# Dense tiles of a hybrid decoder step: the three products as the outermost loop

## What is computed

```python
for layer in range(DEPTH):
    h = rmsnorm(x, norm_mix[layer])
    mix = even_mixer(h, ...) if layer % 2 == 0 else odd_mixer(h, ...)   # each: h @ w_in, mixing, @ w_out
    x = x + mix
    h = rmsnorm(x, norm_mlp[layer])
    x = x + jnp.square(jax.nn.relu(h @ mlp_w_up[layer])) @ mlp_w_down[layer]
y = rmsnorm(x, norm_final)
```

## Time and profile before

| | us |
|---|---|
| median of 3 runs | 3569.35 |
| lowest and highest | 3564.08, 3569.45 |
| the profiled execution | 3563.22 |
| its span, first to last instruction | 3561.4 |
| TensorE busy | 3150.5 (88%) |
| DVE busy | 1233.3 (35%) |
| ACT busy | 742.8 (21%) |
| GpSimd busy | 248.5 (7%) |

### The profile page before, as it was taken

One profiled execution on the slowest core, in us unless ns is written; L12 is line 12 of the kernel. 1 busy time (PEld: TensorE's weight loads), 2 busy tenths in 40 slices (PEclk: granted clock), 3 DMA queues, 4 the chain that ended last, 5 costly groups with the idle time before them and its releaser, 6 DMA issues. The chain is left out here.

```text
span 3561.4 us, 45192 instructions
## 1 busy us (share of the span) xinstructions
PE 3150.5 (88%) x18272; PEld 2946.8 (83%) x18272; DVE 1233.3 (35%) x1537; ACT 742.8 (21%) x1029; POOL 248.5 (7%) x303
## 2 busy tenths in 40 slices
PE   7997788987428899999998999699869899999997
PEld 6996667765318899999998999577649899999996
DVE  5633444325322422222224221644261422222223
ACT  3212211104221311112122000321140311111112
POOL 1001211101000100000001000323000100000000
PEclk9998777767659999999999999666569999999998
DMA  4110000010002111111112111000112111111111
GB/s 133 41 53 12 1 1 0 0 29 24 10 15 92 33 49 46 47 47 47 42 48 82 47 47 36 1 1 0 36 65 95 42 47 42 47 47 47 46 48 48
DMA packets 222442, 141.92 MB, mean 40 GB/s; under 512 B 6419, under 2 KB 218722, under 8 KB 221861
## 3 DMA queue, kind: packets, MB, share of 16 engines
q1 hardware_dynamic: 222380, 141.08, 13.1%
HBM read 120.06 MB, written 21.10 MB: 40 GB/s over the span
## 5 line engine op out<-in xcount | busy, mean ns | idle before, releaser
L161 PE MATMUL ps<-act_hi,w_hi 128*128 128x344 f32 x3072 | 662.0, 324 | 89.9 <-DVE act_lo L382 33.5
L161 PE MATMUL ps<-act_lo,w_hi 128*128 128x344 f32 x3072 | 656.5, 322 | 0.0
L161 PE MATMUL ps<-act_hi,w_lo 128*128 128x344 f32 x3072 | 653.1, 321 | 0.0
L161 PEld LDWEIGHTS ps<-act_hi,w_hi 128*128 128x128 f32 x3072 | 520.7, 189 | 99.4 <-issue 83.5
L161 PEld LDWEIGHTS ps<-act_lo,w_hi 128*128 128x128 f32 x3072 | 524.3, 190 | 0.0
L161 PEld LDWEIGHTS ps<-act_hi,w_lo 128*128 128x128 f32 x3072 | 516.3, 189 | 0.0
L143 ACT ACTIVATE w_hi<-w_raw 128x1024 fp32r<-128x1024 f32 x192 | 202.6, 1055 | 1163.1 <-PE ps L161 1096.5
L567 DVE TENSOR_TENSOR proj<-proj,ps 128x1032 f32 (+1 forms) x80 | 98.4, 1230 | 704.6 <-PE ps L161 704.6
L161 PE MATMUL ps<-hidden_lo,w_hi 128*128 128x344 f32 x1536 | 325.9, 320 | 0.0
L161 PE MATMUL ps<-hidden_hi,w_hi 128*128 128x344 f32 x1536 | 325.8, 320 | 0.0
L161 PE MATMUL ps<-hidden_hi,w_lo 128*128 128x344 f32 x1536 | 324.3, 319 | 0.0
(11 more groups left out here) (322 smaller groups left out, 3156.8 us busy)
## 6 DMA issues: line engine op xcount, KB each, us to landing
w_raw<-mlp_w_up SPq DMA_DIRECT2D x64, 512.0 KB, 4.0
w_raw<-mlp_w_down SPq DMA_DIRECT2D x64, 512.0 KB, 3.6
w_raw<-gla_w_in SPq DMA_DIRECT2D x24, 512.0 KB, 3.8
w_raw<-even_w_in SPq DMA_DIRECT2D x22, 512.0 KB, 3.8
x_save<-proj SPq DMA_DIRECT2D x2, 4128.0 KB, 12.2
proj<-x_save SPq DMA_DIRECT2D x2, 4128.0 KB, 12.8
x_rows<-x_prompt SPq DMA_DIRECT2D x8, 512.0 KB, 3.5
w_raw<-even_w_out SPq DMA_DIRECT2D x8, 512.0 KB, 3.7
```

Source lines behind the costliest of these rows:

```text
L161: last = c.nc.tensor.matmul(c.ps[:, 3 * slot + ch, 0:CW], w[:, slot, k, :], x[:, k, ch * CW:(ch + 1) * CW], start=(k == 0 and n == 0), sto ...
```

## The change

In `multiply_tile` the product becomes the outermost loop, then `k`, then the column chunk. The order of the products becomes high by high, low weights by high activations, high weights by low activations. `ready` is given the pass `n` along with `k`, and its last call is `ready(2, KT)`.

In the norm, `ready` waits in the first pass for `act_hi[k]` (`norm_upper`), does nothing in the second, and in the third issues the sums of squares and waits for `act_lo[k]`, as it did before in the only pass.

In a down tile, `ready` waits in the first pass for seven `hid_hi` at k = 0 and for the eighth at k = 7, and at the start of the third pass for all eight `hid_lo`.

```diff
@@ multiply_tile
-    for k in range(KT):
-        if ready:
-            ready(k)
-        for n, (w, x) in enumerate(((c.w_hi, hi), (c.w_hi, lo), (c.w_lo, hi))):
+    for n, (w, x) in enumerate(((c.w_hi, hi), (c.w_lo, hi), (c.w_hi, lo))):
+        for k in range(KT):
+            if ready:
+                ready(n, k)
             for ch in range(NCH):
                 last = c.nc.tensor.matmul(c.ps[:, 3 * slot + ch, 0:CW], w[:, slot, k, :],
                                           x[:, k, ch * CW:(ch + 1) * CW],
                                           start=(k == 0 and n == 0), stop=(k == KT - 1 and n == 2))
     if ready:
-        ready(KT)
+        ready(2, KT)
     last.then_inc(c.tiles_done, 1)
@@ Norm.on_tensor
-        def ready(k):
+        def ready(n, k):
+            if n == 0:
+                pe.wait_ge(self.upper, KT * self.n0 + k + 1)
+            if n < 2:
+                return
             if k and k % 2 == 0:
                 j = k // 2 - 1
                 pe.wait_ge(self.paired, self.pairs + j + 1)
@@ mlp_phase, do_down on TensorE
-                def ready(k):
-                    if k == 0 or k == KT - 1:
-                        pe.wait_ge(lower, f * KT + (h0 + 2 + (KT - 1 if k == 0 else KT)))
+                def ready(n, k):
+                    if n == 0 and (k == 0 or k == KT - 1):
+                        pe.wait_ge(upper, f * KT + (h0 + (KT - 1 if k == 0 else KT)))
+                    if n == 2 and k == 0:
+                        pe.wait_ge(lower, f * KT + (h0 + 2 + KT))
                 multiply_tile(c, pe, (odd + parity) % 2, g, hid_hi, hid_lo, ready)
```

## The result

| | before | after |
|---|---|---|
| median, us | 3564.8 (5 runs) | 3588.8 (5 runs) |
| lowest and highest, us | 3557.0, 3569.5 | 3585.1, 3590.6 |
| the profiled execution, us | 3563.22 | 3589.55 |
| its span, us | 3561.4 | 3587.2 |

The changed kernel takes 1.0065 times as long, 95% interval 1.0049 to 1.0081: 24 us more. The prediction was 3589, slower, with 0.90 on that side.

A forecast was written before the change was run, and what follows sets the result against it. TensorE was taken as the bound, busy 88% of the span. Down sections 11.5 plus norms 10.4 gave 21.9 us: 3585.1 from the profiled execution, 3591.3 from the median; forecast 3589 between them, range 3575 to 3603.

The forecast's parts named there:

- The stop in the down sections: First down tile of eight sections: TensorE waits 1.34 us for `hid_hi[7]`; with restart 1.44 each, 11.5 us in all.
- the restart: Down sections, after the stop: the next three groups take 0.10 us more.
- The norm: First tile after each of four norms: 2.6 us later each, 10.4 us in all, between 4.0 and 18.
- work left: Norm's first tile: matmuls and all four sums behind the last `act_hi` make Ln 1.0 us later at full clock.
- slow clock: Norm's first tile: 3.5 us at 1.2 GHz behind the last `act_hi`, 1.6 us lost per norm.
- The nearest row: Final phase, as clock evidence for the norm: bursts fill 16.64 of 22 us and the clock stays at 0.50.
- The reordering itself: All 13,824 dense matmuls: order inside a tile costs nothing, as groups begin at equal distances.
- the prediction's own sign: Trace of after: dense groups stay 0.47 us apart; the prediction is wrong if that distance moves at all.
- The rival for the pace: Dense matmuls: order changes pace; 1.6 ns saved each undoes the loss (0.04), or added weight changes cost 15 us (0.05).
- The sum: Whole kernel: 11.5 for down sections plus 10.4 for norms, 21.9 us slower.
- The clock rises early: Norms: first-pass bursts raise the clock, so each costs only 1.0 us; 15.5 in all, time 3582; chance 0.17.
- The norms pay: Norm's first tile: the 2.9 us earlier start is kept, 11.5 us gained against the down sections' 11.5; 3567; chance 0.06.

The follow-up runs named there:

- the run with the clock kept up: Changed kernel plus matmuls on constants into an unused PSUM bank where TensorE waits for `act_hi` in the norm's first tile; 1.0053 of before, 19 us slower.
- the swapped products: Kernel before, k still outermost, only the product order changed to high-high, low weights by high activations, high weights by low activations; 3562.8 us in one execution.

## Why the prediction held, point by point

**The stop in the down sections** was put at 1.34 us and 0.10 for the restart; the trace shows 1.26 to 1.35 and 0.10 to 0.11 in the eight sections. The sum of 11.5 us stands against 12.1 that came back when the down tiles were undone; of these, 64 x 0.013 = 0.8 are the pace. The place of the stop was found by following `hid_hi[7]` through ACT's queue, where the weights' split stands ahead of the copy; the run that swapped the two shortened the stop as that says. The stops cost no clock: PEclk is 1.00 through both MLPs.

**The norm** was put at 2.6 us: 1.0 of work left, and 1.6 of slow clock. Measured are 2.1, 3.2, 2.1 and 2.0, in sum 9.3 against 10.4. The 1.0 is what the run with the clock kept up showed. For the clock I took 3.5 us behind the last `act_hi`; the four norms had 2.5, 4.8, 2.5 and 2.2. At 0.45 us lost for each, that is 1.1, 2.2, 1.1 and 1.0, which with 1.0 gives what was measured. So this execution lies below the term in three norms and above it in one, while the mean over twelve norms, 3.6 us slow and 1.6 lost, is the term itself. The nearest row that I chose for it, the bursts of the final phase, pointed the right way: in none of the twelve norms did the clock rise during the bursts of the first pass. In the first norm it rose 3.5 us after the last pair began at 46.8, where I had reckoned with up to 5.4.

**The reordering itself** was costed at nothing, from equal distances between groups. This step failed in the small: distances that are read to 0.01 us over three matmuls cannot show 0.013 us over 72. Seven splits of weights, six whole tiles apart, can; but no row of the kernel before could tell it ahead, since no tile ran by passes there. By the prediction's own sign (wrong if the dense distance moves at all) this part is wrong: the distance went from 157.87 to 158.05 ns. The rival for the pace was named with the wrong mechanism, as the swapped products showed.

**The sum** was 21.9 us on the profiled execution. The span grew by 25.8: 9.3 and 12.8 in the two places, and the rest where the diff changes nothing or only the pace. The medians differ by 24.0. That the point came out within a microsecond is luck: put between 3585 and 3591, it stands for a kernel before of 3567.1, 2.3 above the median of the five runs, and its sum is 2.1 too small, so two misses cancel.

**The rivals.** "The clock rises early" is out: it came back to 1.00 only 2.2 to 4.8 us behind the last `act_hi` in the four norms, and Ln is 16.3 to 17.5 us behind it, where full clock gives 15.35. "The norms pay" is out: the 2.9 us of earlier start were not kept, and the run with two sums moved into the first pass shows that their place had a part in it, as the rival had said: Ln came 0.7 to 0.9 us sooner than before, still not 2.9. For the pace, the Trainium skill ("TensorE: Matmul & The Clock Gate", section "Wait — 56ns, not 53.3ns?") would have 146 ns, an estimate from its formula. The trace agrees with it in neither order: 24 matmuls of a pass take 3.79 us after (1299.36 to 1303.15), 158 ns each, as before.

## What to carry to other kernels

When a loop order is changed so that a slow operand is wanted late, look for the operand that is wanted sooner in exchange, and follow its writer through its own queue: here the high part of the last hidden tile was wanted 6.6 us earlier, and stood behind another job on ACT. An earlier start is worth something only if the work moved into the gained time is work that the end would else wait for; count what is left behind the last arrival, not the idle time that goes away. And put the step that releases the next stage (here the last sum) ahead of waits that it does not need: this gave 10 us where the reordering lost 24.

## What the runs showed of the hardware

The mixers, which no version here touches, took between 1930.4 and 1943.8 us with the projections around them (whose pace is worth at most 1 us of that) in eleven profiled executions, while the MLPs repeated to 0.1 us where their code was the same. So most of the scatter of this kernel's times, 10 to 15 us from run to run, lies in these stretches. Their length goes with the time for which TensorE's granted clock stood at 0.50 in them: 758 us in the shortest and 795 in the longest, with a correlation of 0.91 over the eleven. That the clock is the cause, and not only a companion, no run here shows. A change of a few us in a dense stage is read better from the stage's own rows than from the total.
